# RMS norms of two FFNs and a K/V/Q projection: the sum of squares formed on GpSimd, with one product with ones on TensorE

## The chip, the cores and the metric

The kernel runs on one core of a Trainium2 chip. The metric is the device time of one execution in microseconds, as the median of several runs.

## What is computed

The reference is a two-block network on one sequence of 512 tokens with 1024 features, in float32. The first block is a modulated hybrid mixer (a long convolution beside an mLSTM) and a mixture of experts. The second block has a gated delta-rule mixer, an FFN (FFN0), a sliding-window attention with its own K/V projection, and a second FFN (FFN1). Only the norms ahead of FFN0, of K/V/Q and of FFN1 concern the change:

```python
def rmsnorm_2(x, g):
    xf = x.astype(jnp.float32)
    y = xf * lax.rsqrt(jnp.mean(xf * xf, axis=-1, keepdims=True) + EPS)
    return (y * g.astype(jnp.float32)).astype(x.dtype)
...
    h = h + conv_ffn(rmsnorm_2(h, f_norm[layer]), f_w_up[layer], ...)      # FFN0, FFN1
...
    kv = rmsnorm_2(h, kv_norm) @ kv_w + kv_b
...
    h = h + swa_sink_attention(rmsnorm_2(h, b_norm[i]), k_sh, v_sh, ...)
...
def conv_ffn(h, w_up, conv_w, conv_b, w_down):
    u = causal_dwconv_2(h @ w_up, conv_w) + conv_b
    gate, up = jnp.split(u, 2, axis=-1)
    return (jax.nn.silu(gate) * up) @ w_down
```

K/V and Q share the mean of squares, since both norms are of the same `h` with other gains.

## The kernel before, in words

Activations are kept transposed: features on the 128 partitions, in KD = 8 slabs of 128 features, tokens (512) along the free dimension. `x` is the residual stream. Weights stream from HBM in units of 2 MB (`wall`) into two slots of `ring`, one unit being eight slabs of 512 output columns, that is four output tiles of 128 columns. Each output tile has a bank of PSUM; unit g uses banks 0 to 3 or 4 to 7 in turn.

Products of float32 are made of three products of rounded parts (`product`, lines 474 to 476): high weight by high activation, high by low, low by high. So an output tile with eight slabs is 24 matmuls of 128x512. ScalarE makes the high part of the weights (`w_hi`, line 1091) and VectorE the low part (`w_lo`, line 1603), one output tile at a time. The high and low part of the activations come from `x_hi` (ScalarE, line 1106) and `x_lo` (VectorE, line 1620). The gain is multiplied in there, and the factor `rstd` of the norm only after the product, when VectorE takes a tile out of PSUM (FFN: line 1785, K: line 1835, Q: line 1853). This lets TensorE start on a layer before its norm is known.

The norm itself (`norm` of each engine): ScalarE squares slab k of `x` into `sq[:, k % 2]` (line 940, 128x512), TensorE multiplies it by a 128x128 matrix of ones and adds the eight in one bank (line 456), which leaves the sum over all features on every partition, and ScalarE turns it into `rstd` by a logarithm and an exponential (lines 929 and 930), then signals `std`. The two halves of `sq` are handed back by `sq_used`. A float32 product with ones shows in the trace as two matmul records.

Order of the work around the change, by hand on each engine:

- TensorE, `first_tile` (line 678): output tile 0 of the first unit of the layer, then the norm's eight products, then `other_tiles`. In the FFN (line 818) these are tiles 1 to 3, then units 1 to 10 of the up projection, then the down projection in two groups of three units each (`down0_0` to `down0_5`). Tile 0 of the first down unit needs its low weights (`w_lo`). In K/V (line 857) the next work is tile 1, then the V part, which has the tokens on the partitions, then a tiny transposition of `rstd` (line 868), then Q.
- ScalarE: the last `x_hi`, one `w_hi`, then `norm`, then in the FFN the loop over units (`unit`, line 1194): per output tile one `w_hi` of the following unit, and for the first two tiles a SiLU (line 1202) of what VectorE has finished. In K/V it makes the eight high parts for Q after the norm, then the high weights of Q.
- VectorE: the last `x_lo`, one `w_lo`, then a wait for `std`. In the FFN its loop (`unit`, line 1764) does per output tile one `w_lo` of the following unit, then four instructions on the tile: times `rstd` (line 1785, into `sq` as scratch) and three steps of the short convolution (lines 1786 to 1788); per unit it adds two products of gate and up (line 1793). After ten units it makes the low parts of 13 hidden tiles (line 1800), then `w_lo` of the first down unit.
- SyncE issues the load of unit u+2 when TensorE has finished unit u.
- GpSimd is used for indirect DMAs of the mixture of experts, and for nothing after it.

The norms are numbered 0 to 7; FFN0's is 4, that of K/V/Q is 5, FFN1's is 6. Norms 0 to 3 and 7 are as they were.

Of the kernel before, what the change touches and what calls it, by code (L numbers as in the profile page):

```python
# [16 lines left out]
ALU = mybir.AluOpType  # L17
# [9 lines left out]
KD = D // P  # L27
# [103 lines left out]
def build(nc, xt_in, wada, wall, wexp, w_if, w_router, w_ab, vecs, rows, b_if, cst_in, ints, att_bias, levels_in, out_t):  # L131
# [5 lines left out]
    with ctx:  # L137
# [5 lines left out]
        def S(name):  # L143
            if name not in sems:
                sems[name] = ctx.enter_context(nc.semaphore(name))
            return sems[name]

        PS = ctx.enter_context(nc.psum_tensor("PS", [P, 8, 512], F32))
# [17 lines left out]
        sq = sb("sq", [P, 2, T])  # L166
        rstd = sb("rstd", [P, T])
# [19 lines left out]
        ident, ones = C("ident"), C("ones")  # L187
# [103 lines left out]
        def freed(eng, g):  # L291

            if g >= 0:
                e, n = EMPTIED[g]
                eng.wait_ge(S({"A": "ev_act", "D": "ev_dve", "X": "xt"}[e]), n)
# [139 lines left out]
        def _(pe):  # L435
            mm = nc.tensor.matmul
# [14 lines left out]

            def norm(n, bank):

                for k in range(KD):
                    pe.wait_ge(S("sq"), KD * n + k + 1)
                    mm(PS[:, bank, :], ones, sq[:, k % 2, :], start=k == 0, stop=k == KD - 1).then_inc(S("sq_used"), 1)  # L456
# [27 lines left out]
            for k in range(KD):  # L484
                last = product(PS[0:64, 4, :], (wif_hi[:, k, :], wif_lo[:, k, :]), (x_r[:, k, :], h_r[:, k, :]), k == 0, k == KD - 1)
            last.then_inc(S("if_mm"), 1)

            for g in range(10):
# [6 lines left out]
                for j in range(4):  # L495
# [4 lines left out]
                    for k in range(KD):  # L500
                        last = product(PS[:, 4 * (g % 2) + j, :], (in_hi(p)[:, k, :], ring_r[:, g % 2, k, j * P:(j + 1) * P]),
                                       (x_r[:, k, :], h_r[:, k, :]), k == 0, k == KD - 1)
# [3 lines left out]
            for t in range(NT):  # L506
                for hd in range(MH):
                    last = nc.tensor.transpose(PS[:, 4 + t, hd * P:(hd + 1) * P], A[:, 16 + hd, t * P:(t + 1) * P], ident)
# [5 lines left out]
            for i in range(CT):  # L514
                last = mm(PS[:, 0, :], ones, A[:, 40 + i, :], start=i == 0, stop=i == CT - 1)
            last.then_inc(S("cl_mm"), 1)
            for i in range(CT):
                pe.wait_ge(S("cl_sq"), i + 1)
                last = mm(PS[:, 2, :], ones, A[:, 4 + i, :], start=i == 0, stop=i == CT - 1)
# [3 lines left out]
            for t in range(NT):  # L523
                last = nc.tensor.transpose(PS[:, 3, 4 * t:4 * t + 4], gr[5][:, t * P:(t + 1) * P], ident[0:4, 0:4])
# [9 lines left out]
            for hd in range(MH):  # L534
# [7 lines left out]
                for s in range(NT):  # L542
                    pe.wait_ge(S("ml_p"), NT * hd + s + 1)
                    mm(PS[:, 6, s * P:T], A[:, 16 + s, hd * P:(hd + 1) * P], A[:, 52 + s, s * P:T], start=s == 0,
                       stop=s == NT - 1)
                    last = mm(PS[:, 7, s * P:T], ones, A[:, 52 + s, s * P:T], start=s == 0, stop=s == NT - 1)
# [24 lines left out]
            for t in range(NT):  # L571
                for k in range(KD):
                    last = mm(PS[:, 0, 64 * t:64 * t + NG + E], h[:, k, t * P:(t + 1) * P], wrt[:, k, :], start=k == 0, stop=k == KD - 1)
            last.then_inc(S("logits"), 1)
            for t in range(NT):
                if t >= 2:
                    pe.wait_ge(S("ht_ev"), t - 1)
                for k in range(KD):
                    last = nc.tensor.transpose(PS[:, 2 + 2 * (t % 2) + k // 4, (k % 4) * P:(k % 4 + 1) * P], h[:, k, t * P:(t + 1) * P], ident)
# [6 lines left out]
            for u in range(NT):  # L586
                last = mm(PS[:, 7, 0:E], ones, asg[2][:, u, :], start=u == 0, stop=u == NT - 1)
            last.then_inc(S("rank"), 1)

            n = pairs(pe)  # L590
# [17 lines left out]
            with pe.Fori(0, n) as i:  # L608
                for p in range(PIECES):
# [11 lines left out]
                    for q in range(2):  # L621
                        k = k0 + q
# [10 lines left out]
                        last = mm(out, x_hi, lo[:, q, :], start=False, stop=final)  # L633
# [41 lines left out]
                            last.then_inc(S("h_free"), 1)  # L675
                    last.then_inc(S("mm"), 1)

            def first_tile(g, split, n):

                name = GROUPS[g][0][0]  # L680
                freed(pe, g - 2)
                pe.wait_ge(S("w_lo"), split_count(UIDX[name], 0))
                for k in range(KD):
                    pe.wait_ge(S("h_lo"), KD * split + k + 1)
                    last = product(PS[:, 4 * (g % 2), :], w_split(unit_slot(name), k, slice(0, P)), h_split(k), k == 0, k == KD - 1)
                last.then_inc(S("mm"), 1)
                freed(pe, g - 1)
                norm(n, NORM_BANK[n])

            def other_tiles(g, tiles):  # L690

                name = GROUPS[g][0][0]
                for j in tiles:
                    pe.wait_ge(S("w_lo"), split_count(UIDX[name], j))
                    for k in range(KD):
                        last = product(PS[:, 4 * (g % 2) + j, :], w_split(unit_slot(name), k, slice(j * P, (j + 1) * P)), h_split(k), k == 0, k == KD - 1)
                    last.then_inc(S("mm"), 1)
# [42 lines left out]
            for c in range(NT):  # L740
                last = mm(PS[:, 0, 8 * c:8 * c + 8], C("tri_incl"), dl[1][:, c, :], start=True, stop=True)
# [76 lines left out]
            def ffn(layer, g_up, g_dn, split, n):  # L818
                u0 = UIDX[f"up{layer}_0"]

                first_tile(g_up, split, n)
                other_tiles(g_up, range(1, 4))
                pe.wait_ge(S("std"), n + 1)
                sgroup(g_up + 1, h_split)
                with pe.Fori(0, (FU - 3) // 2) as i:
                    for j in range(2):

                        pe.wait_ge(S("ev_dve"), 8 * i + EMPTIED[g_up + j][1])
                        for t in range(4):
                            pe.wait_ge(S("w_lo"), 8 * i + split_count(u0 + 2 + j, t))  # L830
                            for k in range(KD):
                                last = product(PS[:, 4 * ((g_up + j) % 2) + t, :], w_split((u0 + j) % 2, k, slice(t * P, (t + 1) * P)), h_split(k), k == 0, k == KD - 1)
                            last.then_inc(S("mm"), 1)
                sgroup(g_up + FU - 1, h_split)

                for m in range(2):
                    g = g_dn + m
                    freed(pe, g - 2)
                    for ui in range(3):
                        u = UIDX[f"down{layer}_{3 * m + ui}"]  # L840
                        nk = 8 if ui < 2 else FT - 16
                        for j in range(4):
                            pe.wait_ge(S("w_lo"), split_count(u, j))
                            for k in range(nk):
                                if m == 0 and j == 0:
                                    pe.wait_ge(S("f_lo"), FT * layer + 8 * ui + k + 1)
                                last = product(PS[:, 4 * (g % 2) + j, :], w_split(u % 2, k, slice(j * P, (j + 1) * P)), (hidden_hi(8 * ui + k), hid_r[:, 8 * ui + k, :]),
                                               ui == 0 and k == 0, ui == 2 and k == nk - 1)
                                if layer == 0 and m == 1 and ui == 2 and j == 3 and k < nk - 1:
                                    last.then_inc(S("h_free"), 1)  # L850
                            last.then_inc(S("mm"), 1)
# [2 lines left out]


            g = G_KV
            first_tile(g, 4, 5)
            other_tiles(g, range(1, 2))
            pe.wait_ge(S("w_lo"), split_count(UIDX["kv"], 3))
            for j in range(2):  # L860
                for t in range(2 * j, 2 * j + 2):
# [1037 lines left out]
        def _(pool):  # L1899
# [41 lines left out]
            for j in range(2):  # L1941
                rwait(pool, S(f"xg{j}"), 16 * n + 16)
                rwait(pool, S(f"idx{j}"), 16 * n + 16)


NORM_BANK = [0, 0, 0, 0, 4, 0, 4, 4]

# [101 lines left out]
```

## Time and profile before

| | us |
|---|---|
| median of 3 runs | 2925.29 |
| lowest and highest | 2923.60, 2925.39 |
| the profiled execution, its own time | 2934.49 |
| span of the profiled execution | 2933.0 |

The span runs from the first to the last instruction in the profile. The profiled execution is 9.2 us longer than the median of the runs. Times in the rows are microseconds from the start of the span unless marked ns. PE is TensorE's matmuls, PEld its weight loads, DVE is VectorE, ACT ScalarE, POOL GpSimd, SP SyncE. Matmuls overlap in their pipeline, so the spacing of their starts says more than the duration of one.

### The profile page before, as it was taken

To read this page: it belongs to the slowest core of one execution; us is meant where nothing else is said; L and a number is where in the kernel's file an instruction comes from. 1 tells how busy PE (TensorE), PEld (TensorE's weight loads), DVE (VectorE), ACT (ScalarE), POOL (GpSimd) and SP (SyncE) were. 2 spreads that over 40 slices of the span, in tenths; PEclk is the share of its full clock that TensorE was granted. 3 is DMA by queue.
4 is the path that set the end of the run, shared out by engine and by line. 5 is a ranking of instruction groups with operands and counts; after the bars stand their busy time and mean duration, and the time that the engine had idled before them with its cause. 6 is when DMAs were issued, how large, how long until landed. Compare 5 with 4: busy or idle time off the path is not lost.

```text
span 2933.0 us, 31459 instructions
## 1 busy us (share of the span) xinstructions
PE 2515.9 (86%) x11452; PEld 1982.6 (68%) x11452; DVE 1798.5 (61%) x2226; ACT 1201.4 (41%) x1531; POOL 127.8 (4%) x144
## 2 busy tenths in 40 slices
PE   4989769839999999957986887699999975999997
PEld 2778424427777777735865877478878765788876
DVE  6877533138888888855735665467772445477742
ACT  3222320128888888844233111442332424422322
POOL 0000000011111222200000000000000000000000
PEclk8989879859999999988997999799999976999999
DMA  7522102059999999831220000022322310122221
GB/s 305 210 77 89 55 0 86 0 212 375 356 364 354 354 363 359 328 133 44 100 86 1 1 1 1 29 86 86 109 91 86 115 58 1 61 111 86 100 101 58
DMA packets 38598, 398.49 MB, mean 136 GB/s; under 512 B 8816, under 2 KB 9200, under 8 KB 15600
## 3 DMA queue, kind: packets, MB, share of 16 engines
q1 hardware_dynamic: 27664, 375.21, 33.7%
q0 software_dynamic: 10848, 22.08, 2.0%
q8 instruction: 61, 1.00, 0.1%
q14 instruction: 25, 0.20, 0.0%
HBM read 388.86 MB, written 21.02 MB: 140 GB/s over the span
## 4 chain that ended last, share of the span: by engine, by line
PE 52%; DVE 16%; ACT 5%; issue 4%; DMA 1%; DVEq 0%; ACTq 0%; POOL 0%; SPq 0%; POOLq 0%
PE PS L474 8%; PE PS L475 8%; PE PS L476 8%; PE PS L631 6%; PE PS L749 6%; PE PS L633 6%; PE PS L632 6%; DVE ring_r L1603 2%; DVE A L1384 2%; ACT w_hi_r L1091 2%; PE PS L456 1%; DVE A L1787 1%; PE PS L597 1%; DVE hid_r L1800 1%; DVE sq L1785 1%
## 5 line engine op out<-in xcount | busy, mean ns | idle before, releaser
L474 PE MATMUL PS<-h_hi_r,w_hi_r 128*128 128x512 f32 x1120 | 440.7, 394 | 34.9 <-DVE h_r L1611 33.5
L1603 DVE TENSOR_TENSOR ring_r<-ring,w_hi_r 128x1024 fp32r<-128x1024 f32 x196 | 238.4, 1223 | 341.6 <-ACT w_hi_r L1091 341.6
L476 PE MATMUL PS<-h_hi_r,ring_r 128*128 128x512 f32 x1120 | 437.7, 391 | 0.0
L475 PE MATMUL PS<-h_r,w_hi_r 128*128 128x512 f32 x1104 | 431.9, 391 | 0.0
L631 PE MATMUL PS<-h_r,top_r 128*128 128x512 f32 x768 | 315.0, 410 | 34.7 <-DVE ring_r L1572 34.7
L1091 ACT ACTIVATE w_hi_r<-ring 128x1024 fp32r<-128x1024 f32 x196 | 201.8, 1050 | 328.0 <-PE PS L476 217.4
L1064 ACT ACTIVATE h_r<-A 128x1024 fp32r<-128x1024 f32 x256 | 266.1, 1059 | 49.5 <-PE PS L633 49.5
L474 PEld LDWEIGHTS PS<-h_hi_r,w_hi_r 128*128 128x128 f32 x1120 | 211.6, 189 | 83.8 <-DVE h_r L1611 34.6
L476 PEld LDWEIGHTS PS<-h_hi_r,ring_r 128*128 128x128 f32 x1120 | 211.7, 189 | 44.6
L475 PEld LDWEIGHTS PS<-h_r,w_hi_r 128*128 128x128 f32 x1104 | 208.7, 189 | 43.7 <-issue 0.7
L1572 DVE TENSOR_TENSOR hid_r<-A,h_r 128x1024 fp32r<-128x1024 f32 x176 | 208.0, 1219 | 24.6 <-ACT h_r L1064 22.6
L631 PEld LDWEIGHTS PS<-h_r,top_r 128*128 128x128 f32 x768 | 146.7, 191 | 78.9 <-DVE ring_r L1572 41.4
L632 PE MATMUL PS<-h_r,h_hi_r 128*128 128x512 f32 x512 | 199.8, 390 | 0.0
L749 PE MATMUL PS<-A 128*128 128x128 f32 x1392 | 168.8, 280 | 17.2 <-DVE A L1734 13.1
L749 PEld LDWEIGHTS PS<-A 128*128 128x128 f32 x1392 | 162.2, 194 | 22.4 <-issue 20.0
L1572 DVE TENSOR_TENSOR ring_r<-ring,h_r 128x1024 fp32r<-128x1024 f32 x128 | 150.5, 1222 | 28.6 <-ACT h_r L1064 27.3
L474 PE MATMUL PS<-x_r,top_r 128*128 128x512 f32 x320 | 129.2, 404 | 14.1 <-DVE mod L1321 9.2
L475 PE MATMUL PS<-hid_r,w_hi_r 128*128 128x512 f32 x352 | 139.1, 395 | 0.0
L633 PE MATMUL PS<-hid_r,top_r 128*128 128x512 f32 x352 | 137.8, 391 | 0.0
L1064 ACT ACTIVATE h_r<-ring 128x1024 fp32r<-128x1024 f32 x128 | 129.0, 1051 | 16.3 <-PE PS L633 15.0
L475 PE MATMUL PS<-h_r,top_r 128*128 128x512 f32 (+1 forms) x328 | 131.7, 401 | 0.0
L476 PE MATMUL PS<-x_r,ring_r 128*128 128x512 f32 x320 | 127.5, 398 | 0.0
(360 smaller groups left out, 4272.4 us busy)
## 6 DMA issues: line engine op xcount, KB each, us to landing
A<-wexp SPq DMA_DIRECT2D x64, 2048.0 KB, 8.8
ring<-wall SPq DMA_DIRECT2D x63, 2048.0 KB, 8.2
ring<-wexp SPq DMA_DIRECT2D x32, 2048.0 KB, 8.8
A<-wada SPq DMA_DIRECT2D x12, 2048.0 KB, 12.0
x<-xt_in SPq DMA_DIRECT2D x2, 2048.0 KB, 14.0
A<-y_assignments SPq DMA_DIRECT2D x4, 1024.0 KB, 7.9
h_tokens<-A SPq DMA_DIRECT2D x4, 512.0 KB, 2.8
A<-att_bias SPq DMA_DIRECT2D x1, 2048.0 KB, 12.6
```

Of the source, the lines that this page charges most:

```text
L474: mm(out, w[0], x_[0], start=first, stop=False)
L475: mm(out, w[0], x_[1], start=False, stop=False)
L476: return mm(out, w[1], x_[0], start=False, stop=last_)
L631: mm(out, x_hi, hi[:, q, :], start=first, stop=False)
L632: mm(out, x_lo, hi[:, q, :], start=False, stop=False)
L633: last = mm(out, x_hi, lo[:, q, :], start=False, stop=final)
L749: last = mm(PS[:, bank + hd // 4, (hd % 4) * P:(hd % 4 + 1) * P], lhs(hd), rhs(hd), start=True, stop=True)
L1064: a_(hi, w, ACT.Copy).then_inc(S("m_hi"), 1)
L1091: a_(w_hi_r[:, :, j * P:(j + 1) * P], ring[:, slot, :, j * P:(j + 1) * P], ACT.Copy).then_inc(S("w_hi"), 1)
L1384: ins = stt(dst[:, s:T], src[:, 0:T - s], w(j), dst[:, s:T], ALU.mult, ALU.add)
L1572: tt(lo, w, hi.bitcast(F32), ALU.subtract).then_inc(S("m_lo"), 1)
L1603: tt(ring_r[:, slot, :, cols], ring[:, slot, :, cols], w_hi_r[:, :, cols].bitcast(F32), ALU.subtract).then_inc(S("w_lo"), 1)
```

## The change

TensorE no longer makes eight products for norms 4, 5 and 6. GpSimd adds the eight squares into `rstd` (which is free at that time), each addition waiting for its square and for the addition before it. TensorE makes one product of this sum with ones. This product stands behind the second output tile instead of behind the first. ScalarE's part is as it was, but the halves of `sq` are now handed back by GpSimd, both with the first addition, and one with each later one but the last; the count is completed by TensorE's product.

```diff
             def norm(n, bank):
+                if n in POOL_SUMS:
+                    pe.wait_ge(S("sq_sum"), POOL_SUMS.index(n) + 1)
+                    mm(PS[:, bank, :], ones, rstd[:], start=True, stop=True).then_inc(S("sq_used"), 1)
+                    return
                 for k in range(KD):
                     pe.wait_ge(S("sq"), KD * n + k + 1)
                     mm(PS[:, bank, :], ones, sq[:, k % 2, :], start=k == 0, stop=k == KD - 1).then_inc(S("sq_used"), 1)
...
-            def first_tile(g, split, n):
+            def first_tiles(g, split, n):
...
                 last.then_inc(S("mm"), 1)
+                other_tiles(g, range(1, 2))
                 freed(pe, g - 1)
                 norm(n, NORM_BANK[n])
...
-                first_tile(g_up, split, n)
-                other_tiles(g_up, range(1, 4))
+                first_tiles(g_up, split, n)
+                other_tiles(g_up, range(2, 4))
...
-            first_tile(g, 4, 5)
-            other_tiles(g, range(1, 2))
+            first_tiles(g, 4, 5)
...
+            for n in POOL_SUMS:
+                pool.wait_ge(S("sq"), KD * n + 2)
+                nc.gpsimd.tensor_tensor(rstd[:], sq[:, 0, :], sq[:, 1, :], ALU.add).then_inc(S("sq_used"), 2)
+                for k in range(2, KD):
+                    pool.wait_ge(S("sq"), KD * n + k + 1)
+                    pool.wait_ge(S("sq_used"), KD * n + k)
+                    last = nc.gpsimd.tensor_tensor(rstd[:], rstd[:], sq[:, k % 2, :], ALU.add)
+                    last.then_inc(S("sq_used" if k < KD - 1 else "sq_sum"), 1)
...
+POOL_SUMS = [4, 5, 6]
```

## Rows read from the trace of the kernel before

**Rows 1.** The page: busy time, share of the span and instructions of each engine

```profile
PE 2515.9 (86%) x11452; PEld 1982.6 (68%) x11452; DVE 1798.5 (61%) x2226; ACT 1201.4 (41%) x1531; POOL 127.8 (4%) x144
```

**Rows 2.** One line, L456: min/median/max ns, start of first and last; who waited for it

```profile
L456 PE MATMUL PS<-sq,cst x128: 591/592/1222, 19.6 to 2917.3; 128*128 128x512 f32 x128
...
  ACT sq L940: 78.8, 48
```

**Rows 3.** Timeline of FFN0's norm: start, duration, engine, line; in brackets idle before and releaser

```profile
1921.14 1.14 ACT L940 ACTIVATE sq<-x 128x512 f32<-128x512 f32 x2
...
1922.59 7.59 PE L456 MATMUL PS<-sq,cst 128*128 128x512 f32 x16
...
1928.38 0.63 ACT L940 ACTIVATE sq<-x 128x512 f32<-128x512 f32 x1 [0.23 <-PE PS L456]
...
1929.62 0.79 PE L474 MATMUL PS<-h_hi_r,w_hi_r 128*128 128x512 f32 x1
...
1930.32 0.69 ACT L929 ACTIVATE rstd<-PS,eps 128x512 f32<-128x512 f32 x1
...
1932.32 0.63 ACT L930 ACTIVATE rstd<-rstd 128x512 f32<-128x512 f32 x1
...
1934.26 1.06 ACT L1091 ACTIVATE w_hi_r<-ring 128x1024 fp32r<-128x1024 f32 x1
...
1935.36 1.23 DVE L1603 TENSOR_TENSOR ring_r<-ring,w_hi_r 128x1024 fp32r<-128x1024 f32 x1 [12.86 <-ACT w_hi_r L1091]
```

**Rows 4.** The same view, VectorE's first step on FFN0's units 0 and 9

```profile
1936.50 0.69 DVE L1785 TENSOR_TENSOR sq<-PS,rstd 128x512 f32<-128x512 f32 x1
...
2135.79 0.69 DVE L1785 TENSOR_TENSOR sq<-PS,rstd 128x512 f32<-128x512 f32 x1
```

**Rows 5.** The chain that ended last, around FFN0's first down unit: start, duration, what

```profile
2147.86 0.70 DVE sq L1785
...
2164.69 1.14 DVE ring_r L1603
```

**Rows 6.** Timeline of the starts of FFN0's first and second down unit

```profile
2164.61 1.22 DVE L1603 TENSOR_TENSOR ring_r<-ring,w_hi_r 128x1024 fp32r<-128x1024 f32 x1
...
2165.93 0.47 PE L474 MATMUL PS<-top_r,w_hi_r 128*128 128x512 f32 x1 [1.78 <-issue]
...
2190.41 4.62 DVE L1603 TENSOR_TENSOR ring_r<-ring,w_hi_r 128x1024 fp32r<-128x1024 f32 x4
...
2191.68 0.79 PE L474 MATMUL PS<-top_r,w_hi_r 128*128 128x512 f32 x1 [3.33 <-DVE ring_r L1603]
```

**Rows 7.** Windows: us, busy of PE, PEld, DVE, ACT, POOL, granted clock, DMA share, GB/s

```profile
1936.00:1956.00 20.00, 20.00 (x90) 16.57 (x89) 14.61 (x20) 5.79 (x7) 0.00 (x0) 1.00 0.29 105
2192.00:2197.50 5.50, 5.50 (x14) 4.24 (x14) 3.03 (x3) 0.00 (x0) 0.00 (x0) 0.50 0.55 235
```

**Rows 8.** Groups of VectorE with two SBUF inputs, by shape: busy us, mean ns, idle before

```profile
L1603 DVE TENSOR_TENSOR ring_r<-ring,w_hi_r 128x1024 fp32r<-128x1024 f32 x164 | 199.5, 1223 | 290.0 <-ACT w_hi_r L1091 290.0
...
L1793 DVE TENSOR_TENSOR A<-A 128x512 f32 x40 | 25.9, 689 | 4.6 <-DVE A L1788 4.6
...
L1884 DVE TENSOR_TENSOR A<-A,sm 128x2048 f32<-128x2048 f32 x6 | 13.8, 2292 | 0.2
```

**Rows 9.** Waits: who waited for whom, us in total, times, longest

```profile
DVE A L1786 <- DVE sq L1785: 8.5, 40, 0.3
...
POOL idx L1915 <- POOL sidx L1930: 26.4, 31, 0.9
```

**Rows 10.** Timeline of the norm of K/V/Q

```profile
2297.86 1.14 ACT L940 ACTIVATE sq<-x 128x512 f32<-128x512 f32 x2
...
2298.66 1.91 PE L456 MATMUL PS<-sq,cst 128*128 128x512 f32 x4
...
2305.72 0.79 PE L474 MATMUL PS<-h_hi_r,w_hi_r 128*128 128x512 f32 x1
...
2323.21 1.05 PE L868 MATMUL PS<-cst,rstd 1*128 1x1 f32 x8
```

## The prediction, made before any run of the changed kernel

> **What bounds the kernel now.** I read the page first: TensorE is busy for 86% of the span, VectorE for 61%, GpSimd for 4% [rows 1]. By that table the norms look like a good target: they take TensorE's time, and GpSimd has nothing to do. A share of the span does not say who sets the end of a stage, so I went to the line of the norm's products. There are 128 records in the kernel, 16 per norm, and ScalarE waits 78.8 us in all for them to give a square back [rows 2]. Three of the eight norms change, 21 of whose 24 products go.
>
> Next, the timeline of FFN0's norm [rows 3]. The first two squares end at 1922.28, the last at 1929.01. The products start at 1922.59, the next output tile at 1929.62: the norm holds TensorE for 7.0 us. The logarithm starts at 1930.32, the exponential ends at 1932.95. Then comes one high part of weights, and VectorE, which has sat idle for 12.86 us, starts at 1935.36. So two chains leave the norm: TensorE's tiles, free at 1929.62, and the chain over `rstd` to VectorE, free at 1935.36.
>
> Which of them sets the end of the FFN? VectorE's first step on unit 0 stands at 1936.50 and on unit 9 at 2135.79 [rows 4]: 199.29 / 9 = 22.14 us per unit. TensorE issues 90 matmuls in 20 us at full clock, 0.222 us each [rows 7], so a unit of 96 takes 21.3 us. The two are close, but TensorE is the faster one, and the loop of VectorE and ScalarE feeds itself: ScalarE's SiLU waits for VectorE, its next high weights follow, and VectorE waits for those. At the end of the up projection TensorE sits idle for 1.78 us until VectorE's low weights, which end at 2165.83, let it start at 2165.93 [rows 6]. The page's chain passes through that VectorE instruction too [rows 5]. It then jumps to TensorE at 2147.86, but the step there is on a tile of unit 9, and TensorE is in unit 10 by then; I take that link for a coincidence of times and the steady 22.14 us for the evidence. **So in both FFNs the end hangs on when `std` comes, not on when TensorE is free.** FFN1 is the same code on the same shapes, and I count it as FFN0.
>
> In K/V it is the other way round: TensorE runs without a gap from 2305.72 to the transposition of `rstd` at 2323.21 [rows 10], long after `rstd` is there. Its own time counts.
>
> **The change part by part.**
>
> *Price of one addition on GpSimd.* The trace has none of this size. From below: VectorE's addition of the same 128x512, 0.69 us. From above: VectorE's of 128x2048, 2.29 us. I take that of 128x1024, 1.22 us, a rate half of VectorE's [rows 8], as the middle one.
>
> The Trainium skill (GPSIMD Engine Reference, Performance versus the Vector engine) has 4497 ns for an addition of 2048 float32, "1.96× slower" than VectorE; as an estimate a quarter of it, 1.12 us. No row here shows it; with it the sum below would be 5.6 us and the time 2930.9.
>
> *Step from one addition to the next.* Each waits for the one before. VectorE's waits for its own result are 0.2 to 0.3 us; GpSimd's wait for its own copy, with some bookkeeping between, is 26.4 / 31 = 0.85 us [rows 9]. I take 0.3, so one step is 1.52 us; bounds 0.9 and 3.13.
>
> *The sum in FFN0.* First addition at 1922.28 + 0.1 = 1922.4, ending at 1923.6. Both halves of `sq` were full, so the third square starts only now: 0.23 to hand back and 0.63 to square [rows 3], about 0.1 to hand on, makes 0.95, and the second addition starts at 1924.55. From there squares keep ahead (a square and its hand-offs are 0.95, a step 1.52). Five steps and the last addition: 7.6 + 1.22. The sum is there at 1933.4, when the last square of before was there at 1929.0: **4.4 us later.**
>
> *TensorE.* The second tile is 24 x 0.222 = 5.3 us, and runs where the products ran, to 1928.1. Then TensorE waits for `sq_sum`, with all its later tiles queued behind, for 5.3 us. An idle stretch of 3.33 us was followed by a granted clock of 0.50 (1.2 GHz) for 5.5 us, one of 1.78 was not [rows 6, 7]. So I expect half clock: 2.75 us lost, of which 0.9 falls on the norm's product (16 records in 7.4 us, so 0.93 us a product, 1.85 at half clock). Tile 2 starts at 1935.3, against 1929.62 + 0.2 + 5.3 = 1935.1 before. The gain of seven products is gone in the wait, and what is left of the half clock makes TensorE some 2 us late. VectorE and the loads, which hang on TensorE's tiles, are later still, so nobody waits for this.
>
> *The chain over `rstd`.* Before, 1.3 us passed from the last square to the logarithm; now from the sum 1.3 + 0.9. `std` and VectorE's start are 1933.4 + 2.2 − 1930.32 = **5.3 us later**. The loading of ScalarE's tables stays hidden in the wait. VectorE carries the 5.3 us through ten units at 22.14.
>
> *What takes some back.* TensorE's wait at the end of the up projection grows from 1.78 to some 5 us, so the first down unit should start at half clock and end 2.75 us later relative to VectorE. That comes out of the wait of 3.33 us before the second down unit, which shrinks to 0.6. After so short a wait the clock should stay at 1.00, where before it was 0.50 for 5.5 us. The second unit then gains 2.75. Net per FFN: 5.3 − 2.75 = **2.55 us later**.
>
> *K/V/Q.* The first additions start at 2299.1, and the same row of them takes 1.22 + 0.95 + 7.6 + 1.22 = 11.0, to 2310.1; with the product TensorE goes on at 2311.95. Before, after tile 1, it was 2305.72 + 0.2 + 5.3 = 2311.2. With the rest of the half clock (2.75 − 0.9): 0.75 + 1.85 = **2.6 us later**. `rstd` comes by 2314.5, so the transposition at 2323 doesn't wait.
>
> *At no cost:* squares on ScalarE (it waits for the sum anyway) and GpSimd's queue, which has nothing behind the additions. VectorE is idle during them, so neither slows the other. If that cover went, an overlap could cost at most one VectorE instruction, 1.22 us.
>
> **Sum:** 2.55 x 2 + 2.6 = 7.7 us on the profiled execution's 2934.49, which is 9.2 above the median of the runs. On the median: 2925.3 + 7.6 = 2932.9. Each 0.1 us more in a step moves the sum by 0.5 in three places, 1.5 us.
>
> **Rivals.**
> 1. *The clock doesn't give back.* The second down unit still starts at half clock, or the first doesn't. For it: the clock does not follow idle time alone that I can see. The FFNs cost 5.3 each: 10.6 + 2.6 = 13.2, 2938.5.
> 2. *GpSimd is fast,* which ends on the other side. Place: the seven additions. With the lower bounds (0.69 and a step of 0.9) the sum is at 1929.2, TensorE waits about 1 us, keeps its clock and resumes 4.9 us earlier. `std` is 0.2 later. TensorE's wait before down is then long (6.9 us), the clock trade gives 2.75 back, net −2.55 per FFN, and K/V gains 4.4: −9.5, 2915.8. It decides below a step of about 1.1. Against it: GpSimd's own wait of 0.85.
> 3. *Near nothing.* A step of 1.4 or a little less gives 0 to 5.8.
> 4. *GpSimd is slow.* At the upper bounds the additions take 21.2 us, FFN 15.5 − 2.75 each, K/V 12.7: 38, 2963. Half of that way is 2948.
> 5. *TensorE sets the end in the FFNs after all.* Then only its lateness of some 2 us counts, and the sum is about as in 3. The idle 1.78 us speaks against it.
>
> **How the numbers follow.** Forecast (4 to 11 us) 0.38, clock not giving back 0.15, fast GpSimd 0.07, near nothing by 3 or 5 0.30, slow GpSimd 0.10. A measurement of this kernel can tell about 0.2%, 5.85 us, from no change. Of the forecast's 0.38 a third (0.13) lies below that; of the 0.30 near nothing, 0.07 is lifted above it where the clock doesn't give back. So slower is 0.25 + 0.15 + 0.10 + 0.07 = 0.57, same 0.13 + 0.23 = 0.36, faster 0.07. The range is 2923 to 2941: below it the fast cases, above it the slow ones.
>
> **What would show it.** In the changed profile: seven additions per norm; read the spacing of their starts, since the Trainium skill (Perfetto Trace Analysis, GPSIMD Engine Instruction) calls the spans of this engine unreliable. Then: a TensorE idle time of about 5 us before the one product; the logarithm 13.3 us after the first squares' end instead of 8.0; VectorE's idle time before its first low weights 18 instead of 12.86; still 22.14 per unit; TensorE's wait before the first down unit near 5, before the second below 1.78, and the clock there at 1.00. I am wrong if VectorE's start moves by less than 3 us, if the spacing is below 1.1 or above 2, or if TensorE no longer waits at the end of the up projection.

## The result and the profile after

The changed kernel takes 2934.89 us (median of 6 runs, 2934.35 to 2936.81), the kernel before 2924.72 us in the runs beside it. The ratio is 1.0034, with an interval of 1.0021 to 1.0047: slower, by 6 to 14 us. The forecast was 2932.9 us in 2923 to 2941.

The page of the changed kernel. GpSimd has 21 instructions more than in [rows 1], and TensorE is busy for 19 us less:

```profile
PE 2496.9 (85%) x11410; PEld 1976.5 (67%) x11410; DVE 1798.1 (61%) x2226; ACT 1200.6 (41%) x1531; POOL 161.4 (6%) x165
```

The timeline of FFN0's norm, in the columns of [rows 3]. In this run the stage begins 4.85 us earlier than in the profile of before, so distances are compared and not positions:

```profile
1916.29 1.14 ACT L944 ACTIVATE sq<-x 128x512 f32<-128x512 f32 x2
...
1917.59 1.28 POOL L1951 TENSOR_TENSOR rstd<-sq 128x512 f32<-128x512 f32 x1 [648.00 <-ACT sq L944]
...
1919.67 8.36 POOL L1955 TENSOR_TENSOR rstd<-rstd,sq 128x512 f32<-128x512 f32 x6 [0.80 <-ACT sq L944]
...
1928.18 1.88 PE L456 MATMUL PS<-rstd,cst 128*128 128x512 f32 x2 [4.84 <-POOL rstd L1955]
...
1930.09 0.69 ACT L933 ACTIVATE rstd<-PS,eps 128x512 f32<-128x512 f32 x1 [2.85 <-PE PS L456]
...
1935.13 1.23 DVE L1607 TENSOR_TENSOR ring_r<-ring,w_hi_r 128x1024 fp32r<-128x1024 f32 x1 [17.48 <-ACT w_hi_r L1095]
```

The seven additions take from 1917.59 to 1928.03, TensorE waits 4.84 us for them and then makes one product where eight stood. The logarithm starts 12.66 us after the first two squares end (1917.43); before it was 8.04 us. VectorE's idle time has grown from 12.86 to 17.48 us. Its pace over the units is the old one, as the counterparts of [rows 4] show, (2135.59 − 1936.27) / 9 = 22.15 us:

```profile
1936.27 0.68 DVE L1789 TENSOR_TENSOR sq<-PS,rstd 128x512 f32<-128x512 f32 x1
...
2135.59 0.68 DVE L1789 TENSOR_TENSOR sq<-PS,rstd 128x512 f32<-128x512 f32 x1
```

The starts of FFN0's first and second down unit, against [rows 6]:

```profile
2165.75 0.76 PE L478 MATMUL PS<-top_r,w_hi_r 128*128 128x512 f32 x1 [6.33 <-issue]
...
2191.49 0.50 PE L478 MATMUL PS<-top_r,w_hi_r 128*128 128x512 f32 x1 [1.37 <-DVE ring_r L1607]
```

TensorE's wait before the first down unit is 6.33 us where it was 1.78, the one before the second 1.37 where it was 3.33. The granted clock, in the columns of [rows 7], behind each of the two waits and behind the wait for GpSimd:

```profile
1928.20:1931.60 3.40, 3.40 (x7) 1.99 (x8) 0.00 (x0) 1.49 (x2) 0.00 (x0) 0.52 0.02 5
2165.80:2170.80 5.00, 5.00 (x12) 3.94 (x13) 3.25 (x5) 1.58 (x2) 0.00 (x0) 0.51 0.07 30
2191.50:2197.00 5.50, 5.50 (x24) 4.58 (x25) 3.34 (x3) 0.00 (x0) 0.00 (x0) 1.00 0.87 346
```

The half clock has moved from the second down unit to the first, where TensorE has a reserve: the second unit starts 25.74 us behind the first, and 25.75 before. The product records count it: 24 in 5.5 us against 14 in [rows 7].

The stages can be cut at VectorE's last addition to the residual ahead of each norm, which lies before everything that the change touches (not before everything that the kernels with early squares touch, see there). Lengths in us from one such addition to the next; "to down 1" is from the cut to the start of the first down unit of FFN0, "to scores" from the cut to attention's first score:

| kernel | FFN0 | K/V/Q and attention | FFN1 | to down 1 | to scores | attention, its mean clock |
|---|---|---|---|---|---|---|
| before | 376.7 | 241.2 | 373.8 | 247.1 | 73.9 | 108.6, 0.65 |
| before, again | 376.7 | 241.2 | 373.8 | 247.1 | 73.9 | 108.6, 0.65 |
| changed | 378.6 | 242.6 | 375.8 | 251.8 | 74.7 | 110.6, 0.63 |
| changed, again | 378.7 | 242.7 | 375.9 | 251.8 | 74.7 | 110.7, 0.61 |
| e_order | 379.3 | 242.0 | 376.4 | 252.5 | 73.8 | 109.4, 0.64 |
| e_first | 381.3 | 243.3 | 378.4 | 252.9 | 79.7 | 104.8, 0.69 |
| e_dve | 373.4 | 241.8 | 370.5 | 246.6 | 68.6 | 115.2, 0.59 |
| e_dve, again | 373.5 | 231.5 | 370.7 | 246.6 | 68.6 | 104.9, 0.73 |
| e_kvq | 376.7 | 242.1 | 371.0 | 247.0 | 74.8 | 109.4, 0.65 |
| e_ffn | 378.5 | 241.2 | 377.4 | 251.7 | 73.9 | 108.6, 0.65 |
| e_warm | 380.0 | 243.1 | 377.4 | 251.6 | 75.7 | 108.6, 0.65 |
| e_early | 369.7 | 239.8 | 367.2 | 241.6 | 70.8 | 109.1, 0.67 |
| e_early, again | 371.4 | 243.9 | 368.5 | 241.7 | 70.8 | 114.0, 0.60 |
| e_two | 370.4 | 236.5 | 366.3 | 240.6 | 68.1 | 109.4, 0.65 |

By the profiles the change costs 1.9 + 1.5 + 2.0 us, 5.3 before rounding. Behind the last cut all kernels take 22.4 to 22.5 us alike.

### The profile page after: what moved, and what is told of

It is laid out like the page before. It is cut to its first block, busy times and chain, and to the rows that moved or that the text cites. A ratio compares the mean times of both kernels' runs of the same rounds, so it can differ in the third digit from the quotient of the medians.

```text
span 2933.5 us, 31419 instructions
## 1 busy us (share of the span) xinstructions
PE 2496.9 (85%) x11410; PEld 1976.5 (67%) x11410; DVE 1798.1 (61%) x2226; ACT 1200.6 (41%) x1531; POOL 161.4 (6%) x165
## 4 chain that ended last, share of the span: by engine, by line
PE 44%; DVE 20%; ACT 7%; issue 5%; DMA 1%; POOL 1%; DVEq 1%; ACTq 0%; POOLq 0%; SPq 0%
PE PS L635 6%; PE PS L637 6%; PE PS L636 6%; PE PS L754 6%; PE PS L478 5%; PE PS L479 5%; PE PS L480 5%; DVE ring_r L1607 3%; ACT w_hi_r L1095 3%; DVE A L1791 2%; DVE A L1388 2%; DVE sq L1789 2%; DVE A L1792 2%; DVE A L1790 1%; PE PS L601 1%
## 5 line engine op out<-in xcount | busy, mean ns | idle before, releaser
L480 PEld LDWEIGHTS PS<-h_hi_r,ring_r 128*128 128x128 f32 x1120 | 211.2, 189 | 44.4
L1206 ACT ACTIVATE A<-A 128x512 f32<-128x512 f32 x44 | 27.8, 632 | 320.7 <-DVE A L1792 320.7
```

Of the source, the lines that this page charges most:

```text
L480: return mm(out, w[1], x_[0], start=False, stop=last_)
```

## The experiments

The theory: `std` sets the end of both FFNs, through VectorE; TensorE sets the end of K/V/Q; and the clock gives part of the FFNs' loss back. The main rival: TensorE sets the end of the FFNs too. A timed run of the kernel before takes anything from 2921 to 2936 us, so the profiles' stages carry more of the verdicts than the times.

**The kernel before, once more** (no edit)

> The kernel before, once more, as a control. The changed kernel's runs lie at 2934.4 to 2936.8, those of before at 2921.2 to 2932.0 with a profiled one at 2934.5. Stage by stage the two profiles differ by 5.3 us after FFN0's first squares and by -4.85 us ahead of them, where nothing was changed. Theory A (the part ahead of FFN0 scatters by some 5 us from run to run): ratio to before 1.000, and this profile starts FFN0's squares somewhere between 1912 and 1922 us, while the stages behind it repeat those of before within 1 us (376.7, 241.2, 356.2 us from norm to norm). Rival (the stages behind scatter): they differ from these by several us.

Ratio 1.0001 (0.9990 to 1.0013). The stages repeat within 0.1 us (table). The first cut lies at 1917.7 us, in the first profile at 1918.9, in the changed kernel's at 1914.0 and in `e_order`'s at 1921.3, with nothing changed ahead of it. So a span isn't compared as a whole. The 12 timed runs lie between 2923.4 us at a mean granted clock of 0.924 and 2936.1 us at 0.918: their scatter goes with TensorE's clock.

**Only the move behind the second tile** (`e_order`)

```diff
-POOL_SUMS = [4, 5, 6]
+POOL_SUMS = []
```

> Only the move: eight products on TensorE as before, but behind the second output tile; no addition on GpSimd. Theory A (the chain over rstd sets the end of the FFNs): rstd comes 5.4 us later than before, VectorE's start too, 22.14 us per unit stay, TensorE's wait before the first down unit is 1.78 + 5.4 = 7.2 us, the half clock moves from the second down unit to the first and gives 2.7 back: each FFN +2.7 us, K/V/Q 0, sum +5.4 us, ratio 1.002 to before. Rival B (TensorE sets the end of the FFNs): TensorE's work is the same, nothing moves, ratio 1.000.

Ratio 1.0036 (1.0024 to 1.0049), 2941.7 us. Stages +2.6, +0.8, +2.6 us. The logarithm starts 13.5 us after the first squares' end, 5.45 us later than before; the first down unit starts 5.4 us later, and TensorE waits 6.71 us for it:

```profile
1923.60 1.13 ACT L944 ACTIVATE sq<-x 128x512 f32<-128x512 f32 x2
...
1938.22 0.69 ACT L933 ACTIVATE rstd<-PS,eps 128x512 f32<-128x512 f32 x1
...
2173.80 0.77 PE L478 MATMUL PS<-top_r,w_hi_r 128*128 128x512 f32 x1 [6.71 <-issue]
```

TensorE does the same work as before without one wait more in the norm, and the FFNs are longer. That rules out that TensorE's work alone sets their end. The size, 2.6 of 5.4, is what the clock leaves. K/V/Q up to the scores is unmoved (73.8), as TensorE's path should be. The ratio asks for 10.5 us, more than the 6.0 of the stages, of which more below.

**The product behind the first tile** (`e_first`)

```diff
-                other_tiles(g, range(1, 2))
                 freed(pe, g - 1)
                 norm(n, NORM_BANK[n])
+                other_tiles(g, range(1, 2))
```

> As the changed kernel, but the one product stands behind the first output tile, so TensorE waits for the sum with one tile less done. Theory A: rstd comes when it does in the changed kernel (12.7 us from the first squares' end to the logarithm), VectorE's start too. TensorE is 5.4 us later than in the changed kernel, so its wait before the first down unit is about 1 us, the clock stays full there and is half again before the second: each FFN 2.7 us longer than in the changed kernel, K/V/Q 5.4 us longer: +16 us on before, ratio 1.0055. Without the clock (only the chain over rstd counts) +10.7. Rival B: each of the three places 5.4 us longer than in the changed kernel, +21 us on before.

Ratio 1.0065 (1.0052 to 1.0078), 2947.1 us. The interval holds the 1.0055 of theory A and the rival's +21 us (1.0072) too, so the stages have to decide. FFNs +4.6 each, K/V/Q to the scores +5.8. TensorE waits 10.18 us for the sum, but the wait before the first down unit is down to 1.25:

```profile
1932.42 2.04 PE L456 MATMUL PS<-rstd,cst 128*128 128x512 f32 x2 [10.18 <-POOL rstd L1955]
...
2171.24 0.47 PE L478 MATMUL PS<-top_r,w_hi_r 128*128 128x512 f32 x1 [1.25 <-issue]
```

By the rival each FFN should grow by another 5.4 us; it is 2.7. This is what theory A forecast, but only 1.6 us of it come behind the start of the second down unit, where the clock is at half again, for 3.4 us. The other 1.1 come through TensorE: `rstd` comes when it does in the changed kernel (within 0.1 us), yet VectorE's first step on unit 2 stands 45.5 us behind that on unit 0, where in the changed kernel it is 44.4. TensorE's finished units set when loads are issued, and in `e_first` ScalarE waits long for the weights, here 7.38 us against 1.86 in the changed kernel:

```profile
1982.64 1.28 ACT L1095 ACT_TABLE_LOAD   x1 [7.38 <-DMA ring<-wall]
```

```profile
1972.22 1.28 ACT L1095 ACT_TABLE_LOAD   x1 [1.86 <-DMA ring<-wall]
```

So TensorE's slack in the FFNs is finite: of its 5.4 us, some 4 are absorbed, and the rest reaches VectorE by way of the loads. The second tile was worth its place in K/V/Q alone (5.0 us), and attention took most of that back (104.8 us instead of 110.6).

**VectorE adds** (`e_dve`, and once more as `r_dve`)

```diff
-                nc.gpsimd.tensor_tensor(rstd[:], sq[:, 0, :], sq[:, 1, :], ALU.add)...
+                sum_squares(4 + 2 * layer)      # the same additions on VectorE, ahead of its wait for std
...
+            sum_squares(5)                      # ahead of its low parts for Q
```

> As the changed kernel, but VectorE makes the seven additions (0.69 us each, 0.2 to 0.3 us for its own result) instead of GpSimd. Theory A: a step is 0.95 us, as one square on ScalarE was before, so rstd is within 0.5 us of before. TensorE is 4.5 us earlier. Each FFN gains only by the clock, 2 to 2.7 us, K/V/Q gains 4 us: -9 us, ratio 0.997. Rival B: TensorE's 4.5 us count in all three places, -13.5 us, ratio 0.9954. If the additions interfere with TensorE or ScalarE the squares are further apart than 0.95 us.

> The kernel with VectorE's additions once more, for a second profile of its attention. In the first, the scores started 5.3 us earlier than before and attention then took 115.2 us at a mean clock of 0.59, where before it took 108.6 at 0.65 in both profiles, so that the gain was lost. Theory A (the clock in attention depends on where its idle stretches fall, not on the additions): some other length between 105 and 115 us. Rival (the gain is always lost, as when attention is bound by something else): 115 us at 0.59 again, the end of attention at the same place.

Ratios 0.9986 (0.9976 to 0.9997) and 0.9971 (0.9958 to 0.9984). FFNs −3.3 and −3.2 us, scores 5.3 us earlier. The additions are 0.80 us apart ((4.67 − 0.69) / 5):

```profile
1925.14 4.67 DVE L1643 TENSOR_TENSOR rstd<-rstd,sq 128x512 f32<-128x512 f32 x6 [0.76 <-ACT sq L944]
...
1931.09 0.69 ACT L933 ACTIVATE rstd<-PS,eps 128x512 f32<-128x512 f32 x1 [0.84 <-PE PS L456]
```

This is the forecast's rival of a fast adder, with another engine in its place. Its logarithm is 0.5 us earlier than before, and the rest of the 3.3 is the clock. The same kernel's attention was profiled twice (windows from the first score to the last output copy):

```profile
2362.13:2477.28 115.15, 84.91 (x464) 70.48 (x464) 59.09 (x72) 45.15 (x145) 0.00 (x0) 0.59 0.04 17
```

```profile
2362.22:2467.11 104.89, 69.89 (x464) 58.24 (x464) 59.06 (x72) 45.15 (x145) 0.00 (x0) 0.73 0.05 18
```

The same 464 matmuls and the same work on VectorE and ScalarE take 10.3 us more at a lower clock. So the first profile's lost gain in K/V/Q was no bound of attention.

**The two halves of the change** (`e_kvq`, `e_ffn`)

```diff
-                other_tiles(g, range(1, 2))
+                if n in POOL_SUMS:
+                    other_tiles(g, range(1, 2))
                 freed(pe, g - 1)
                 norm(n, NORM_BANK[n])
+                if n not in POOL_SUMS:
+                    other_tiles(g, range(1, 2))
...
-POOL_SUMS = [4, 5, 6]
+POOL_SUMS = [5]         # e_kvq; [4, 6] in e_ffn
```

> Only the norm of K/V/Q changed; both FFNs as before. Theory A: the scores of attention start 0.9 us later than before, as in the changed kernel (72.4 us behind the squares, 71.6 before). What attention then takes is set by the clock that TensorE is granted in it, not by the change: 104.8 us at a mean clock of 0.69 to 115.2 us at 0.59 in the profiles so far. Ratio to before 1.000 within 0.002. Rival: attention takes the same in each kernel and the differences seen are the change's; then it lasts 110.5 us as in the changed kernel, with a clock of 0.63, and the ratio is 1.001.

> Only the norms of the FFNs changed, K/V/Q as before. Theory A: from norm to norm FFN0 and FFN1 are 1.9 to 2.0 us longer than before, and 22.14 us per unit stay; with the changed kernel's +8 to +10 us in the timed runs the FFNs account for about 4 of them: ratio 1.0014. If nearly all of the +8 to +10 comes with the FFNs (1.003), some of it is not in the stages that the profiles show.

Ratios 1.0004 (0.9988 to 1.0020) and 1.0006 (0.9996 to 1.0017), both too wide to tell 2 us from 5. They also can't be added up against 1.0034: the 30 runs of before beside these kernels, `e_warm` and the first of `e_early` have a median of 2932.05 us, where it was 2924.72 beside the changed kernel. In the profiles K/V/Q alone has the scores 0.9 us later and leaves FFN0 as it was; the FFNs alone leave K/V/Q at 241.2. Attention takes 109.4 us in `e_kvq`, between the 108.6 of before and the 110.6 of the changed kernel, which settles nothing between its theory and rival. FFN0 is +1.8 in `e_ffn`, as expected, FFN1 +3.6, more than expected: there the clock falls again on the second down unit, behind a wait of only 2.28 us (a mean of 0.69 in the window below), so 1.1 us come back and not 2.8:

```profile
2811.60:2817.10 5.50, 5.50 (x17) 4.34 (x18) 3.32 (x3) 0.00 (x0) 0.00 (x0) 0.69 0.76 322
```

And FFN1 in `e_kvq`, where its code is that of before, is 2.8 us *shorter*: a wait of 3.35 us stands before the second down unit (before 3.33), but the clock stays full behind it:

```profile
2808.61 0.50 PE L478 MATMUL PS<-top_r,w_hi_r 128*128 128x512 f32 x1 [3.35 <-DVE ring_r L1610]
```

```profile
2808.70:2814.20 5.50, 5.50 (x25) 4.54 (x26) 3.26 (x3) 0.00 (x0) 0.00 (x0) 1.00 0.59 253
```

That is 25 matmuls where [rows 7] has 14. A wait of 3.3 us doesn't always cost the clock, and one of 2.28 can.

**TensorE kept busy before the first down unit** (`e_warm`)

```diff
                     freed(pe, g - 2)
+                    if m == 0:
+                        for _ in range(5):
+                            mm(PS[:, 4 * (g % 2), :], ones, x[:, 0, :], start=True, stop=True)
```

> The changed kernel with five added products of ones (fp32, 0.93 us each, their result overwritten) on TensorE in its wait before the first down unit. Theory A (the clock gives back): TensorE's idle time there falls from 6.33 to about 1.7 us, the clock stays full, the first down unit ends in time, the wait before the second is 3.33 us again and the second starts at half clock: each FFN is 4.6 us longer than before, 2.7 longer than in the changed kernel; sum +5.4 on the changed kernel, ratio 1.0045 to before. Rival (the clock has no part, the changed kernel's FFNs are +1.9 for another reason): same as the changed kernel.

Ratio 1.0028 (1.0016 to 1.0040), where 1.0045 was forecast. FFN0 is 1.4 us longer than in the changed kernel and FFN1 1.6; 2.7 was expected. The mechanism shows: both waits are as forecast, and the half clock is back behind the second:

```profile
2165.93 0.50 PE L478 MATMUL PS<-top_r,w_hi_r 128*128 128x512 f32 x1 [1.90 <-DVE ring_r L1610]
...
2191.71 0.79 PE L478 MATMUL PS<-top_r,w_hi_r 128*128 128x512 f32 x1 [3.31 <-DVE ring_r L1610]
```

```profile
2191.70:2196.00 4.30, 4.29 (x12) 3.44 (x13) 3.37 (x3) 0.00 (x0) 0.00 (x0) 0.62 0.81 347
```

It lasts 3.4 us this time, not 6.8, hence half the price. That the trade happens is shown; its price is 1.4 to 2.8 us.

**The changed kernel, once more** (no edit)

> The changed kernel once more. Its stages from last residual to last residual were +1.9, +1.5 and +1.9 us on before, sum +5.3, while its six timed runs were 8 to 10 us above before; the two parts of the change by themselves gave 1.0006 and 1.0004. Theory A (5.3 us is the change, the rest is scatter of the clock in stages that it doesn't touch): ratio 1.002 here, the FFN stages of the profile +1.9 each again. Rival (something outside these stages belongs to the change): ratio 1.0034 again.

Ratio 1.0032 (1.0020 to 1.0044), 2939.8 us against 2929.0. The stages repeat (+2.0, +1.5, +2.1), so my theory that the rest is scatter of the runs fell: the timed difference is 6 to 13 us, and the stages have 5.3 to 5.6. Since all kernels take the same time behind the last cut, what is missing lies ahead of the first one or in a course of the stages that no profile caught.

**Squares made early** (`e_early`, once more as `r_early`, and `e_two`)

```diff
+            squares(4, range(4))                      # ScalarE; slabs 0 to 3 are ready one unit ahead
             for j in range(3):
                 w_hi(u + 2, j)
+                squares(4, range(4 + j, 5 + j))
             x_hi(4, "f_norm", 0, free=0)
             w_hi(u + 2, 3)
-            norm(4)
+            norm(4, 7)                                # the eighth square alone; alike for norms 5 and 6
...
-                other_tiles(g, range(1, 2))           # the product is behind the first tile again
                 freed(pe, g - 1)
                 norm(n, NORM_BANK[n])
+                other_tiles(g, range(1, 2))
...
-                    mm(PS[:, bank, :], ones, rstd[:], start=True, stop=True)...      # e_two only
+                    mm(PS[:, bank, :], ones, rstd[:], start=True, stop=False)
+                    pe.wait_ge(S("sq"), KD * n + KD)
+                    mm(PS[:, bank, :], ones, sq[:, 1, :], start=False, stop=True)...
```

> The changed kernel with seven of the eight squares made early, each when its slab of x is ready, between the high parts of the weights on ScalarE; GpSimd adds them as they come; only the eighth square, one addition (1.3 us) and the product of ones, here behind the first output tile, are left after the last slab. Theory A: the logarithm starts 3.2 us behind the start of the last square, where it was 9.2 us behind the start of the first two before: 6 us earlier, TensorE resumes 5.5 us earlier. Each FFN 5.5 to 6 us shorter than before, the scores of attention 5.5 us earlier: -17 us, ratio 0.994, give or take what attention's clock does (5 us either way). Rival: the squares hold up ScalarE's high weights or GpSimd and VectorE slow each other while both read SBUF; then the stages ahead of the norms grow by several us and additions take over 1.3 us.

> The kernel with early squares once more, on the chip and beside the runs that its variant is compared with. Expected 0.9969 to before again (0.9953 to 0.9986 then), FFN stages 6 to 7 us shorter than before.

> The kernel with early squares, but GpSimd adds only the first seven, which are all there early, and TensorE makes two products, one of this sum and one of the eighth square. After the last slab no addition of GpSimd is waited for. Theory: TensorE doesn't wait (1.67 us before) and spends 0.93 us more, so the logarithm comes 0.6 us earlier than with early squares and one product: 0.6 us in each of three places, -1.8 us against that kernel, ratio 0.9963 to before. Rival: the first product must wait for GpSimd's seventh addition, then nothing is gained.

`e_early`: 0.9969 (0.9953 to 0.9986) and 0.9973 (0.9963 to 0.9983). `e_two`: 0.9966 (0.9953 to 0.9979), 2918.6 us. Both beat the kernel before and the changed one. `e_two` gains what was forecast (0.9963), `e_early` half of it: 0.994 lies outside both of its intervals. With early squares the first down unit of FFN0 starts 5.5 us earlier than before, and the FFNs are 5.3 to 7 us shorter (5.3 the second time, where 6 to 7 were forecast). The scores come only 3.1 us earlier, not 5.5: in part because TensorE went on at half clock in K/V/Q behind a wait of 1.66 us for the sum (another of 0.97 us stands 2.6 us ahead of it), while in FFN0 it kept full clock behind one of 1.67. The windows behind the two:

```profile
2290.80:2294.10 3.30, 3.30 (x9) 2.21 (x8) 0.00 (x0) 2.30 (x3) 0.00 (x0) 0.50 0.00 0
1920.60:1924.00 3.40, 3.40 (x14) 2.47 (x15) 0.00 (x0) 2.29 (x3) 0.00 (x0) 1.00 0.02 5
```

In `e_two` the logarithm is another 1.0 us earlier (0.6 expected) and the scores 2.7 us, without half clock; against `e_early` by time that is within the intervals. All additions but the last are off the path now, at 1894 to 1911 us (in `e_two` that last one is gone); but they no longer take what they took:

```profile
1893.64 1.29 POOL L1964 TENSOR_TENSOR rstd<-sq 128x512 f32<-128x512 f32 x1 [623.59 <-ACT sq L941]
...
1901.13 1.82 POOL L1968 TENSOR_TENSOR rstd<-rstd,sq 128x512 f32<-128x512 f32 x1 [2.68 <-ACT sq L941]
...
1918.62 1.78 POOL L1968 TENSOR_TENSOR rstd<-rstd,sq 128x512 f32<-128x512 f32 x1 [7.43 <-ACT sq L951]
...
1920.54 1.10 PE L456 MATMUL PS<-rstd,cst 128*128 128x512 f32 x2 [1.67 <-POOL rstd L1968]
```

VectorE's timeline over the same moments:

```profile
1900.57 1.23 DVE L1620 TENSOR_TENSOR ring_r<-ring,w_hi_r 128x1024 fp32r<-128x1024 f32 x1 [3.11 <-ACT w_hi_r L1102]
...
1918.06 1.23 DVE L1620 TENSOR_TENSOR ring_r<-ring,w_hi_r 128x1024 fp32r<-128x1024 f32 x1 [0.20 <-ACT w_hi_r L1102]
```

Where an addition on GpSimd begins 0.56 us into such an instruction of VectorE, which reads two operands from SBUF, it takes 1.8 instead of 1.28 us; VectorE's keeps its 1.23. The Trainium skill (SBUF — State Buffer, Summary: rules for kernel authors) says that such a pair contends and that the second to issue fully blocks until the first finishes. By that rule the addition would lose all of the remaining 0.67 us; it lost 0.50 to 0.54.

The other order costs VectorE. One of its low-weight instructions that begins 1.18 us into an addition takes 1.73 us instead of 1.23:

```profile
2274.57 1.82 POOL L1968 TENSOR_TENSOR rstd<-rstd,sq 128x512 f32<-128x512 f32 x1 [2.54 <-ACT sq L941]
...
2275.75 1.73 DVE L1620 TENSOR_TENSOR ring_r<-ring,w_hi_r 128x1024 fp32r<-128x1024 f32 x1
```

And ahead of each norm one of seven low parts of the activations, begun 0.58 us into an addition, takes 1.79 us instead of 0.74. The seven, in `e_early` and before:

```profile
1909.94 5.77 DVE L1637 SCALAR_TENSOR_TENSOR h_r<-x,vec,h_hi_r 128x512 fp32r<-128x512 f32 x7
```

```profile
1914.21 4.72 DVE L1620 SCALAR_TENSOR_TENSOR h_r<-x,vec,h_hi_r 128x512 fp32r<-128x512 f32 x7
```

VectorE's last addition to the residual stands right behind them and so comes 1.05 us later, in `e_early` and in `e_two`, ahead of all three norms. So this part of the rival in `e_early`'s forecast came true, at 1 us per norm. FFN0's is ahead of the first cut, and the table leaves it out.

## Why the prediction held, point by point

- **Which chain sets the end.** Right, and it carried the forecast. 22.15 us per unit, the longer wait at the end of the up projection, and above all `e_order`: `rstd` 5.4 us later with TensorE's work unchanged made the FFNs longer. `e_first` shows the limit: 5.4 us more on TensorE brought it onto the path for 1.1.
- **Price of an addition.** Taken 1.22 us with a step of 1.52; measured 1.26 to 1.29 with a step of 1.42 ((8.36 − 1.26) / 5). The start of the second addition was 2.08 us behind the first (2.17). The whole sum took 10.4 us, not 11.0. The wait on its own result costs GpSimd 0.14 us here, not 0.3. The spans of these additions can be used: 1.26 to 1.29 and 0.14 of idle time are the spacing of the starts. The estimate from the Trainium skill (GPSIMD Engine Reference, Performance versus the Vector engine) for one, 1.12 us, was under the measured one by 0.14 to 0.17.
- **The shift of `rstd`.** 4.6 us later, not 5.3: 0.6 by the step.
- **Half clock behind the wait for the sum.** It came (0.52), but in FFN0 it was shorter than forecast, 3.4 us from 0.2 us behind the wait on, so it cost 1.7 us and not 2.75. TensorE reached the end of the up projection about 0.1 us later than before, where I had 2.
- **What the clock gives back.** Right in kind. Forecast 2.75 us per FFN; measured 4.6 − 1.9 = 2.7. `e_kvq`, `e_ffn` and `e_warm` show that it is a matter of 0 to 2.8 us, and not certain. That the forecast's full 2.75 came in both FFNs is in part luck.
- **FFN net.** 2.55 forecast, 1.9 and 2.0 measured; nearly all of the difference is the step.
- **K/V/Q.** The scores come 0.85 us later, where I had 2.6. Two terms were too big: the step of the additions, and the half clock, which I took as 5.5 us from the product on; TensorE's idle time used up the first 3 us of it, and from the product on it ran from 2306.8 to 2310.6, 3.8 us. What I had not is attention: 110.6 and 110.7 us in the changed kernel's profiles, 108.6 in both of before; 1.4 of the 2 us come back behind it, so the stage grows by 1.5.
- **The sum.** Forecast 7.7 us, by the stages 5.3, by the timed runs 6 to 14. The forecast's own terms measured 1.9 + 2.0 + 0.85, 4.7 us. By the stages the outcome is that of the forecast's rival 3 (0 to 5.8 us at a step of 1.4 or a little less; it was 1.42). That the middle of the forecast lies near the timed 10 us is luck: its terms were too big by 3 us, and what it didn't have in it, 0.6 us behind the scores and the part below, made up for that.

**What stays open** is the 4 to 5 us between the stages and the times. The runs give a hint: both profiled executions of before lie at a mean clock of 0.919 and at 2933.3 and 2934.5 us, high among its timed runs, of which the quick ones have 0.922 to 0.924. The changed kernel's 12 runs all lie between 0.915 and 0.920. So the changed kernel seems to miss a favourable course of the clock that the kernel before often has, and attention, at 104.8 to 115.2 us for the same work, has room for it, as has the part ahead of the first cut, which scatters by 7 us (1914.0 to 1921.3). Two things on record fit this. `e_warm`'s timed difference, against runs of before half of which lie above 2932 us, is that of its stages: 8.2 us by the ratio, 3.3 + 1.9 + 3.6 = 8.8 in the table. And three of the ten runs of `e_kvq` have the quick course (2925 to 2927 us at 0.922 to 0.923), so its half of the change doesn't rule it out. But no profile caught a quick execution of before, so where it gains isn't shown.

## What to carry to other kernels

Before work is taken off the busiest engine, find which chain crosses the next meeting point last; here seven products saved on TensorE were worth nothing in the FFNs, since the products' result was awaited elsewhere, and the new adder delivered it 4.6 us later. To take a reduction off the path, start it early rather than give it to an idle engine: four of the eight slabs were ready a unit before, and only the last came at the end. Look then at what the early work runs beside: here it held VectorE up by 1 us per norm. And where a stage has many short waits, its length is a draw of the clock worth several us; compare stages and repeat profiles before a few us are ascribed to an edit.

## What the runs showed of the hardware that I had not expected

- TensorE's idle stretches of 3.31 to 3.35 us before the second down unit were followed by half clock for 6.8 us (before), for 3.4 us (`e_warm`) or not at all (`e_kvq`, FFN1, and `e_early`, FFN0). One of 2.28 us was followed by half clock (`e_ffn`, FFN1), and of two of 1.66 and 1.67 us in `e_early` one was, the one with a wait of 0.97 us shortly ahead of it.
- The same attention, 464 matmuls, took 115.2 us at a mean granted clock of 0.59 and 104.9 us at 0.73 in two profiles of one kernel.
- An addition of 128x512 on GpSimd went from 1.28 to 1.8 us when it began 0.56 us into an instruction of VectorE with two SBUF operands, and VectorE's was not slowed. Where the addition had begun first, VectorE's was: from 0.74 to 1.79 us, and from 1.23 to 1.73.
